# The first 128 columns of x loaded and transposed apart from the next 128, with a shorter warm-up, in a two-block transformer kernel

## What is computed

```
def rms_norm(x, g):
    xf = x.astype(F32)
    y = xf * lax.rsqrt(jnp.mean(xf * xf, axis=-1, keepdims=True) + EPS)
    return (y * g.astype(F32)).astype(x.dtype)
...
    h = x
    for i in range(DEPTH):
        hn = rms_norm(h, norm_mix[i])
            mix = gla_mixer(hn, gla_w_in[j], ...)
```

## Time and profile before

| what | value |
|---|---|
| median of three executions | 889.75 us |
| profiled execution, span from its first to its last instruction | 888.3 us |
| time around the span, by the median | 1.45 us |
| TensorE busy | 883.2 us (99%) |
| VectorE busy | 671.3 us (76%) |
| ScalarE busy | 503.3 us (57%) |
| share of the chain that ended last on TensorE | 96% |
| first matmul of unit 1 | 6.94 us after the span's start |

### The profile page before, as it was taken

How to read it: one execution, slowest core, us unless ns; L and a number is a source line. 1 busy time by engine, 2 the same in 40 slices (tenths; PEclk the granted TensorE clock), 3 DMA queues, 4 the chain that set the end, 5 groups by cost and what they waited for, 6 DMA issues and landing times.

```text
span 888.3 us, 12034 instructions
## 1 busy us (share of the span) xinstructions
PE 883.2 (99%) x4292; PEld 729.1 (82%) x4292; DVE 671.3 (76%) x1039; ACT 503.3 (57%) x822; POOL 75.4 (8%) x88
## 2 busy tenths in 40 slices
PE   9999999999999999999999999999999999999998
PEld 8988888888888878778888888888888888887777
DVE  6997688666746699997786666646879987789763
ACT  7656464444535576887564444444765444577581
POOL 1002000000000403111100000000010000115200
PEclk9999999999999999999999999999999999999999
DMA  9754578776666666433387667665787774857501
GB/s 341 263 179 176 203 260 297 251 267 246 241 213 237 213 227 246 144 103 112 131 300 265 250 235 255 244 233 178 254 296 261 239 245 144 300 175 238 186 26 48
DMA packets 85059, 193.72 MB, mean 218 GB/s; under 512 B 7236, under 2 KB 38340, under 8 KB 85000
## 3 DMA queue, kind: packets, MB, share of 16 engines
q1 hardware_dynamic: 83544, 189.15, 60.3%
q0 software_dynamic: 1024, 3.15, 1.0%
q10 hardware_dynamic: 432, 0.66, 0.2%
HBM read 174.84 MB, written 18.09 MB: 217 GB/s over the span
## 4 chain that ended last, share of the span: by engine, by line
PE 96%; DVE 1%; DMA 1%; ACT 0%; issue 0%; DVEq 0%; ACTq 0%
PE bank L1867 86%; PE bank L1905 3%; PE bank L2156 1%; PE bank L2182 1%; PE bank L2262 1%; PE bank L2292 1%; PE bank L1920 1%; DMA h<-x_dram 0%; DMA h_land<-residual_blocks 0%; PE bank L2167 0%; PE bank L2248 0%; PE bank L2067 0%; PE bank L2071 0%; PE bank L2142 0%; PE bank L2272 0%
## 5 line engine op out<-in xcount | busy, mean ns | idle before, releaser
L1130 DVE TENSOR_TENSOR wlo<-raw,whi 128x1024 fp32r<-128x1024 f32 x295 | 346.5, 1212 | 34.4 <-ACT whi L719 34.1
L719 ACT ACTIVATE whi<-raw 128x1024 fp32r<-128x1024 f32 x295 | 301.6, 1059 | 114.5 <-PE bank L1867 98.6
L1867 PE MATMUL bank<-whi,x_hi 128*128 128x512 f32 x560 | 152.4, 394 | 0.0
L1867 PE MATMUL bank<-wlo,x_hi 128*128 128x512 f32 x560 | 149.9, 389 | 0.0
L1867 PE MATMUL bank<-whi,x_lo 128*128 128x512 f32 x560 | 149.8, 389 | 0.0
L1867 PEld LDWEIGHTS bank<-wlo,x_hi 128*128 128x128 f32 x560 | 105.1, 188 | 22.2
L1867 PEld LDWEIGHTS bank<-whi,x_lo 128*128 128x128 f32 x560 | 105.1, 188 | 21.9
L1867 PEld LDWEIGHTS bank<-whi,x_hi 128*128 128x128 f32 x560 | 103.6, 188 | 22.5 <-issue 1.8
L1867 PE MATMUL bank<-whi,y_hi 128*128 128x512 f32 x396 | 107.6, 393 | 0.1
L1867 PE MATMUL bank<-whi,y_lo 128*128 128x512 f32 x396 | 106.1, 390 | 0.0
L1867 PE MATMUL bank<-wlo,y_hi 128*128 128x512 f32 x396 | 106.0, 389 | 0.0
(11 more groups left out here) (260 smaller groups left out, 888.0 us busy)
## 6 DMA issues: line engine op xcount, KB each, us to landing
raw<-stream_dram SPq DMA_DIRECT2D x295, 512.0 KB, 4.6
ffn_blocks<-ffn_blk SPq DMA_DIRECT2D x22, 256.0 KB, 2.2
ffn_land<-ffn_blocks SPq DMA_DIRECT2D x22, 256.0 KB, 4.1
residual_blocks<-h_blk SPq DMA_DIRECT2D x20, 256.0 KB, 2.0
h_land<-residual_blocks SPq DMA_DIRECT2D x20, 256.0 KB, 2.8
cv_blocks<-cv_blk SPq DMA_DIRECT2D x7, 256.0 KB, 3.6
cv_land<-cv_blocks SPq DMA_DIRECT2D x7, 256.0 KB, 3.2
h_blocks<-h_blk SPq DMA_DIRECT2D x3, 512.0 KB, 2.9
```

The costliest lines, as they stand in the source:

```text
L719: A(whi[:, u % RING, :], raw[:, u % SLOTS, :], ACT.Copy).then_inc(sem("w_hi"), 1)
L1130: V.tensor_tensor(wlo[:, u % SLOTS, :], raw[:, u % SLOTS, :], whi[:, u % RING, :].bitcast(F32), ALU.subtract).then_inc(sem("w_lo"), 1)
L1867: last = T.matmul(bank[pair + t][:, :], lhs[a][:, kt, t * P:(t + 1) * P], w[:, place(w, u), kk * NW:(kk + 1) * NW], start=part != 1 and k ...
```

## The change

x's first 256 columns come in three loads instead of one. Block 0 (128 columns) of the first 128 rows is the first load on SyncE's queue and that of the other 128 rows the first on ScalarE's queue, 64 KB each; together they signal `x_block`. Block 1, 128 KB, comes behind `cols` on SyncE's queue and signals `x_in0`. The loads that stood first on ScalarE's queue, and those behind on SyncE's, are each issued one place later.

Block 0 is transposed into bank 3 and block 1 into bank 4 (`X0_BANK`), with a signal for each (`x_turned`, `lhs_filled`), and VectorE makes `x_hi` of a block as soon as its own transposes are done. Both banks are entered in `free` as released by `lhs`. The warm-up becomes three matmuls of 256 columns, and the two behind the transposes become one of 128 columns between the two pairs of transposes. Three semaphores of VectorE (`df_eps`, `cv_pad`, `mb_eps`) become one (`dve_const`), which counts 1, 2, 3 at the same places.

```
-WARM, KEEP = 4, 2
+WARM = 3
...
+        X0_BANK = (3, 4)
...
         @block.sync
         def _(sp):
-            for n in range(KT // 2):
+            sp.dma_start(h[:, 0, 0:P], x[0:P, 0:P]).then_inc(sem("x_block"), 16)
+            sp.dma_start(cols[:, :], cols_d).then_inc(sem("cols_in"), 16)
+            sp.dma_start(h[:, :, P:2 * P], x[:, P:2 * P].rearrange("(t p) d -> p t d", p=P)).then_inc(sem("x_in0"), 16)
+            for n in range(1, KT // 2):
...
-                if n == 0:
-                    sp.dma_start(cols[:, :], cols_d).then_inc(sem("cols_in"), 16)
-                elif n < PACE - 1:
+                if n < PACE - 1:
...
+            nc.scalar.dma_start(h[:, 1, 0:P], x[P:2 * P, 0:P]).then_inc(sem("x_block"), 16)
             nc.scalar.dma_start(raw[:, 1, 0:NW], stream[1][:, 0:NW]).then_inc(sem("raw_first"), 16)
...
-            dve.wait_ge(sem("lhs_filled"), 1)
             for k in range(2):
-                V.tensor_scalar(X[0][:, k, :], bank[T_BANKS[0]][:, k * SEQ:(k + 1) * SEQ], norm_gain(0)(k), None,
+                dve.wait_ge(sem(("x_turned", "lhs_filled")[k]), 1)
+                V.tensor_scalar(X[0][:, k, :], bank[X0_BANK[k]][:, 0:SEQ], norm_gain(0)(k), None,
                                 ALU.mult).then_inc(sem(("x_first", "lhs_hi")[k]), 1)
...
-            need = x_T(0)
-            for n in range(KEEP):
-                T.matmul(bank[1][:, 0:SEQ], warm[:, 0:P], warm[:, :], start=True, stop=True)
+            for k in range(2):
+                if k == 0:
+                    pe.wait_ge(sem("x_block"), 2 * 16)
+                else:
+                    T.matmul(bank[1][:, 0:P], warm[:, 0:P], warm[:, 0:P], start=True, stop=True)
+                    pe.wait_ge(sem("x_in0"), 16)
+                for t in range(TT):
+                    last = T.transpose(bank[X0_BANK[k]][:, t * P:(t + 1) * P], h[:, t, k * P:(k + 1) * P], ident)
+                last.then_inc(sem(("x_turned", "lhs_filled")[k]), 1)
+            free[X0_BANK[0]] = free[X0_BANK[1]] = ("lhs", c.up("lhs"))
+            need = [("lhs", 1)]
```

More of the change, by code:

```diff
@@ L820, in _ @@
                 if n < 3:
+                    if n == 1:
+                        act.wait_ge(sem("x_block"), 2 * 16)
                     for k in (2 * n - 2, 2 * n - 1):
@@ L1231, in _ @@
             dve.wait_ge(sem("cols_in"), 16)
-            dve.wait_ge(sem("lhs_filled"), 1)
             for k in range(2):
-                V.tensor_scalar(X[0][:, k, :], bank[T_BANKS[0]][:, k * SEQ:(k + 1) * SEQ], norm_gain(0)(k), None,
+                dve.wait_ge(sem(("x_turned", "lhs_filled")[k]), 1)
+                V.tensor_scalar(X[0][:, k, :], bank[X0_BANK[k]][:, 0:SEQ], norm_gain(0)(k), None,
                                 ALU.mult).then_inc(sem(("x_first", "lhs_hi")[k]), 1)
             for n in range(KT // 2):
-                lhs_lo(X, norm_gain(0), (T_BANKS[n],))
-                if n == 0:
+                if n:
+                    lhs_lo(X, norm_gain(0), (T_BANKS[n],))
+                else:
+                    c.wait(dve, "lhs_hi", c.up("lhs_hi"))
+                    for k in range(2):
+                        last = V.scalar_tensor_tensor(X[1][:, k, :], bank[X0_BANK[k]][:, 0:SEQ], norm_gain(0)(k),
+                                                      X[0][:, k, :].bitcast(F32), ALU.mult, ALU.subtract)
+                    last.then_inc(sem("lhs"), 1)
                     dve.wait_ge(sem("w_hi"), 1)
@@ L1509, in _ @@
             HD2 = DF_HD // 2
-            V.memset(dsq65[:, :, :, DF_HD:DF_HD + 1], DF_HD * EPS).then_inc(sem("df_eps"), 1)
+            V.memset(dsq65[:, :, :, DF_HD:DF_HD + 1], DF_HD * EPS).then_inc(sem("dve_const"), 1)
             lrow = rows[:, R_LAM:R_LAM + 4 * DF_HD].rearrange("p (a b e) -> p a b e", a=2, b=2)
@@ L1606, in _ @@
             dve.wait_ge(sem("df_rot"), 4)
-            dve.wait_ge(sem("df_eps"), 1)
+            dve.wait_ge(sem("dve_const"), 1)
             for u, step, arg in df_order("dve"):
@@ L1630, in _ @@
             ffn(1, Y)
-            V.memset(cu[:, :, 0:CONV_K - 1], 0.0).then_inc(sem("cv_pad"), 1)
+            V.memset(cu[:, :, 0:CONV_K - 1], 0.0).then_inc(sem("dve_const"), 1)
             def conv_product(t):
@@ L1686, in conv_parts @@
                                 Y[0][:, bass.ds(blk, 1), :].bitcast(F32), ALU.subtract).then_inc(sem("cv_lhs"), 1)
-            dve.wait_ge(sem("cv_pad"), 1)
+            dve.wait_ge(sem("dve_const"), 2)
             conv_product(CV_IN)
@@ L1709, in _ @@
             second_lo(7, X, "mb", END[MB_IN])
-            V.memset(msq65[:, :, :, MB_HD:MB_HD + 1], MB_HD * EPS).then_inc(sem("mb_eps"), 1)
+            V.memset(msq65[:, :, :, MB_HD:MB_HD + 1], MB_HD * EPS).then_inc(sem("dve_const"), 1)
             V.tensor_copy(mgain[:, 0:1], cols[:, C_QG:C_QG + 1])
             V.tensor_scalar(mgain[:, 1:2], cols[:, C_KG:C_KG + 1], MB_HD ** 0.5, None, ALU.mult).then_inc(sem("mb_gain"), 1)
-            dve.wait_ge(sem("mb_eps"), 1)
+            dve.wait_ge(sem("dve_const"), 3)
             def mb_max(hd):
```

## The result

The changed kernel took 892.99 us at the median of eight executions (891.95 to 893.40), the kernel before 889.91 in eight beside it. The ratio is 1.003 with a 95% interval of 1.0021 to 1.0039. In a later group of five executions it took 892.85 against 890.04, ratio 1.0031 (1.0019 to 1.0044). That is 3 us more; I had said 890.7, with a range of 889.6 to 893.2, so the measured time lies inside the range, close to its upper end.

The account below looks back on a forecast made before the run. TensorE, busy 883.2 of 888.3 us, was taken as the bound. The span 888.3 + 1.10 (later start) - 0.18 (shorter unit 1) + 1.45 (span to median) = 890.67 us, range 889.6 to 893.2.

Parts of the forecast that it names:

- the case that I held likeliest: The bank's wait binds at unit 1 with the clock up in time: chance 0.57, 890.7 us, own range 889.9 to 891.5.
- Two of my own signs of being wrong: Signs listed: unit 1 starts before 7.4, the clock is low beyond its start, or a later wait swallows the shift.
- The new wait on bank 3: Unit 1's first matmul waits for both x_lo of x's first 256 columns, starting at 8.04 instead of 6.94, +1.10 us.
- The landing of block 1: Block 1's load, third on SyncE's queue, was taken to land at 5.7 us, with 5.1 to 6.4 kept.
- The bound by turns of packets: DMA engines alternate between queues by the packet; by that alone block 1 lands at 6.1, shift 1.3 us.
- the one by bytes: Counting bytes over both queues, block 1 is in when 558 KB, or 814 KB, have come: 5.3 to 6.1 us.
- The clock, counted at zero: TensorE's clock was taken to rise before unit 1 at 8.0, so the shorter warm-up added zero.
- The rival I gave 0.30: Late clock, chance 0.30: TensorE at 1.2 GHz when unit 1 starts, 891.6 to 894.5 us, middle 892.8.
- That nothing later takes the shift up: After unit 1 no later wait absorbs the shift; from 20 us on all lies the same 0.9 us later.
- The give-back of unit 1: Unit 1 shortens from 3.49 to 3.31 us with x_lo and both halves of whi ready ahead: -0.18 us.
- The cover of ScalarE's x_hi: Second load's x_hi is done by 10.73, unit 2 wants it not before 11.35: cover 0.6 us, no cost.
- faster* rival: If the bank's wait did not bind, unit 1 starts at 5.8 to 6.5: 889.3 to 888.6 us, chance 0.02.

Follow-up runs that it names:

- e5: Kernel before with the new wait alone (bank 3 entered as released by lhs), one load, full warm-up: 891.04 us, ratio 1.0011.
- e1: Changed kernel with two 256-column warm-up matmuls instead of one of 128 between the transpose pairs, two more behind the second pair: 891.00 us, ratio 1.0009.
- e10: Changed kernel with two 256-column warm-up matmuls instead of one of 128 between the transpose pairs, nothing behind the second pair: 891.00 us, ratio 1.0014.
- e2: Changed kernel with block 0 transposed into bank 6 instead of 3, so no wait for x_lo: 890.43 us, ratio 1.0.
- e6: Kernel before with the three-part load alone, all four transposes into bank 4 behind both loads, a fifth warm-up matmul: 890.38 us, ratio 1.0009.
- e4: Changed kernel with block 0 in bank 6, two 256-column warm-up matmuls between the transpose pairs, one behind the second: 889.98 us, ratio 0.9999.
- e9: Changed kernel run once more, unaltered, against the kernel before: 892.85 us, ratio 1.0031.
- e11: Kernel before with every warm-up matmul replaced by transposes, sixteen ahead of x's transposes and eight behind: 889.91 us, ratio 1.0.

## Why the prediction held in its range and missed in its likeliest case

The time fell inside the range, but not by the case that I held likeliest, and partly by luck. Two of my own signs of being wrong appeared: the clock was low beyond the start of unit 1, and later waits took up a part of the shift. These two errors have opposite signs. Without the 0.85 us that was given back, which I had ruled out, the time would have been about 893.8, outside the range.

*The new wait on bank 3* was right, in place and size. The chain goes from block 1 over two transposes to `x_hi`, both `x_lo` and unit 1. From landing to first matmul I had 2.34 us, the profile 2.22. e5 prices it alone at 1.1 us in the time.

*The landing of block 1* was too early: 5.7 taken, 6.38 measured, at the late end of my 5.1 to 6.4; in the eight profiles with these loads block 1 landed 4.3 to 4.8 us after its issue at 1.64, that is at 5.9 to 6.45. The bound by turns of packets, 6.1, was the better guide than the one by bytes. With it the start moved by 1.66 us and not 1.10.

*The clock, counted at zero*, is the step that failed. I argued that the first 3.8 us lost only one matmul. What I left out of the sum is that TensorE idles from 4.96 to 6.42 and from 7.11 to 8.60, with the clock still low. Unit 1 took 5.68 us instead of the 3.31 of my sum: 2.4 us, against a price of 3.3 for a wholly low unit in the rival. The rival I gave 0.30 is what happened. e1 confirms it by removing it, for 2.0 us at the median, and e10 does so in about half of its executions.

*That nothing later takes the shift up* was wrong by 0.85 us in the profiles: 3.85 at unit 2 became 3.00. In e1, e2, e5 and e6 too the end moved less than unit 2 did. 0.3 of it is the wait for VectorE at 323.6 us and 0.5 the one at 805.8, both shown above. I had read the chain only up to 30 us.

*The give-back of unit 1*, counted at 0.18 us, was about 0.08 where the clock was up: unit 1 took 3.41 us in e1 and e10, not 3.31.

The sum with the measured terms: 1.66 + 2.19 (unit 1, 5.68 - 3.49) - 0.85 = 3.00, in the span; the medians say 3.08.

*The cover of ScalarE's x_hi* held: in the changed kernel it was done at 12.40, ahead of unit 2 at 14.28. The *faster* rival's reason, though, was incomplete: e4 started unit 1 earlier and gained nothing, since in its profile the chain from the weights of unit 2 set the next start.

How much of the late clock is due to the shorter warm-up and how much to the gaps can't be given as two numbers: they do not add (the wait costs 1.0 us with the gaps filled, e1 less e4, and 2.6 with them open, changed less e2). None of the versions beats the kernel before by more than a measurement tells.

## What to carry to other kernels

A buffer chosen for an early step can be one that the next step writes: look up every bank in the table of waits, since a free choice of bank here put three VectorE operations on the path. Price a start-up by TensorE's idle gaps, not only by the work that remains: dummy work in the gaps cost nothing here and was worth 2 us. Look at all executions, not only at the profiled one: the profile of e10 is one in which the clock stayed up. And before moving the first operand forward, look at what the second unit waits for; in e4 its weights' load already ended the gain.

## What the runs showed of the hardware

In the changed kernel a load of 64 KB at the head of an empty queue landed 2.0 to 2.2 us after its issue, while 128 KB, third on its queue and issued 0.9 us behind the first, took 4.7. In e9 the clock of TensorE fell from 2.4 to 1.2 GHz inside a running unit, about 1 us after work had resumed, following idle stretches of 1.02 and 1.49 us with 0.44 us of work between them. Two executions of the changed program differed by 1.4 us: in one the clock rose ahead of unit 1 and fell inside it, in the other it rose only at 13.7 us, and a load landed 0.4 us sooner in the first. In e11 the clock was up from unit 1's first matmul on after nothing but fp32 transposes.
